# A hybrid decoder kernel: the attention norm's inverse square root is shared between GpSimd and VectorE, and the searches for the weight maxima are placed elsewhere

## The chip, the cores and the metric

The kernel runs on one core of a Trainium2 chip. The metric is the device time of one execution in microseconds (us); the median of several executions counts. The core has a matrix engine (TensorE, PE in the profile), VectorE (DVE), ScalarE (ACT), GpSimd (POOL), and SyncE (SP), which only issues transfers here. Every engine works through its own queue in order, and they wait for each other through semaphores.

## The reference, cut to what matters

Two layers, each with sliding-window attention (part A) and retention (part B) side by side, for 2048 prompt tokens and 8 x 4 sample tokens. What the change touches is the norm of the attention's queries and keys, and nothing else that is computed:

```
def rms_norm(x, g=None):
    y = xf * lax.rsqrt(jnp.mean(xf * xf, axis=-1, keepdims=True) + EPS)
...
    qa = rotary(rms_norm(qa.reshape(N, T, A_HEADS, A_HEAD_DIM), q_norm_g), pos, A_ROT_DIM, ROPE_THETA_A)
    ka = rotary(rms_norm(ka.reshape(N, T, A_KV_HEADS, A_HEAD_DIM), k_norm_g), pos, A_ROT_DIM, ROPE_THETA_A)
```

A token has 8 query heads and 2 key heads of 64 values, so ten means of squares per token: one number in each of ten columns, 128 tokens on 128 partitions. The weight maxima are not in the reference. The kernel splits each float32 matrix into two float16 parts (high and low) after scaling it by its largest absolute value, and needs that maximum before it can convert a block of weights.

## The kernel before, in words

A layer has four blocks of weights in this order: A (attention's projection), B0 and B1 (two retention heads each), and O (the output projection). Each block is one stage, and each stage runs over 17 steps: 16 tiles of 128 prompt tokens and one step of 32 sample tokens (step 0 in A, step 2 in the others). The order on every engine is written out by hand. Weights of the next block are searched for their maximum, scaled and converted on VectorE and ScalarE during the stage before, in eight rows of 128 x 1024 (1280 for A).

**An attention step on VectorE** is `a_step` (L1443). For tile s, with t = s - 1 and u = s - 2: the low halves of t's turned queries and keys (`a_lo`, L1022, the instruction at L1027 last), landing s's queries (`a_land_q`), low halves of u's probabilities (`a_plo`), masks and row maxima of t's scores (`a_softmax`, L1096), landing s's keys with the sums of squares (`a_land_k`, L972), and then s's norm, woven into the eight instructions that mix u's heads (`a_mix_head`, L1171). It ends with `a_rotate` (L1002: product with the norm at L1007, rotary to L1019), the gate (L1039), `a_plo` of t (L1053) and, from step 8 to 15, the low halves of one row of B0's weights (`w_low`, L924). TensorE needs L1027 for its scores (L640) and L1019 for its transposes (L604); SyncE turns the probabilities with a transposing DMA (`r<-r`, L2218) after `a_plo`.

**The norm's chain** has 12 links on VectorE, each waiting for the one before: mean plus epsilon (L994), then `rsqrt_link` (L877): an integer shift (L881, with x times -0.5 beside it, L882), the magic constant (L884), and three Newton rounds of three instructions (L886, L888, L890). In steps 0 to 2 the chain stands by itself (`a_norm`); from step 3 its links lie between the heads. `Chain` counts the links on a semaphore:

```
def __call__(self, ins):
    self.put(ins)
    self.wait()
```

**The weight maxima**: `w_absmax` (L901) reduces one row to a column (L907), `w_top` (L911) reduces the eight columns (L915, L918), GpSimd combines the partitions (`share_max`, L2109, the reduction at L2112), and `w_scale` (L927, from L931) makes the scales. In attention B0's rows are searched behind steps 4 (rows 0, 1), 5 (2 to 4) and 6 (5 to 7), with the top behind step 6 and the scales behind step 7. In retention the next block's rows are searched behind the gate of step 3 (rows 0 to 3), behind step 4 (4, 5) and behind step 5 (6, 7, and the top).

**A retention step on VectorE** is `b_step` (L1577): rotary (L1200 to L1211), decay of the scores (L1222), gate (L1039, which waits for ScalarE's tanh, L1831), state (L1264), norm and mix (L1274 to L1282). Around the sample step the order is written out (L1597 to L1610): rotary of the sample S, its gate, decay of T1, `b_vbd` (L1234), rotary of T2, state of T1, decay of S, mix of T1, gate of T2, four `w_absmax`, `b_sum` (L1241), state of S (L1254), mix of S. TensorE waits for L1254 before the scores of T2 (L704) and for L1222 before each output (L724).

**GpSimd's queue** holds the weight loads and the eight `share_max`. `attend` (L2120) issues B0's rows 0 to 3 at its c = 2 and rows 4 to 7 at c = 3, one straight after the other, as nothing stands between them; the c = 2 entry waits, in layer 0, for the eighth turned tile and, in both layers, for a piece count of VectorE that is reached by the end of the previous stage. `share_max` for B0 stands at c = 6.

Of the kernel before, what the change touches and what calls it, by code (L numbers as in the profile page):

```python
# [36 lines left out]
P = 128  # L37
# [25 lines left out]
RSQRT1_LINKS = 2 + 2 * NEWTON  # L63

# [133 lines left out]
def trunk(nc, x_prompt, x_sample, cache_k, cache_v, state_ret, w_in, w_out, norm_g, q_g, k_g, sinks,  # L198
          rope_ap, rope_as, rope_bp, rope_bs, mask_a, mask_s, decay, decay_s, cols, ident,
          y_p, y_s, nk_p, nv_p, nst_p, nk_s, nv_s, nst_s, mixed):  # L200
    with ExitStack() as ctx:
# [27 lines left out]
        ones = sb("ones", [P, KT])  # L229
        g_cur = sb("g_cur", [P, KT])  # L230
# [111 lines left out]

        ch_wm, ch_ws = sem("chain_w_max"), sem("chain_w_scale")
# [520 lines left out]
        def _(v):  # L864
# [12 lines left out]
            def rsqrt_link(ch, x, y, t, i):  # L877

                ch.wait()
                if i == 0:  # L880
                    ch.put(V.tensor_scalar(y.bitcast(I32), x.bitcast(I32), 1, None, ALU.logical_shift_right))  # L881
                    V.tensor_scalar(x, x, -0.5, None, ALU.mult)  # L882
                elif i == 1:
                    ch.put(V.tensor_scalar(y.bitcast(I32), y.bitcast(I32), -1.0, MAGIC, ALU.mult, ALU.add))  # L884
                elif i % 3 == 2:
                    ch.put(V.tensor_tensor(t, y, y, ALU.mult))  # L886
                elif i % 3 == 0:
                    ch.put(V.tensor_tensor(t, t, x, ALU.mult))  # L888
                else:
                    ch.put(V.scalar_tensor_tensor(out=y, in0=t, scalar=1.5, in1=y, op0=ALU.add, op1=ALU.mult))  # L890

# [80 lines left out]
            def a_land_k(L, s):  # L972

                r, b = s.rows, s.par
                ch = Chain(v, ch_an, 4 + RSQRT_LINKS, an(L, s))
# [13 lines left out]
            def a_norm_link(s, ch, i):  # L989

                r, b = s.rows, s.par
                if i == 0:
                    ch.wait()
                    ch.put(V.tensor_scalar(ss[0:r, :], ss[0:r, :], 1.0 / A_DIM, EPS, ALU.mult, ALU.add))  # L994
                else:
                    rsqrt_link(ch, ss[0:r, :], rs[0:r, b, :], rt[0:r, :], i - 1)

            def a_norm(s, ch):
                for i in range(RSQRT_LINKS + 1):
                    a_norm_link(s, ch, i)  # L1000
# [417 lines left out]
            def layer(L, last):  # L1418
# [4 lines left out]
                def a_first(s):  # L1423

                    if s.sample:
# [3 lines left out]
                        a_norm(s, ch)  # L1429
# [8 lines left out]
                    a_norm(s, ch)  # L1438
# [4 lines left out]
                def a_step(s, k=None):  # L1443
# [26 lines left out]
                    if not u.sample:  # L1470
                        a_mix_open(L, u, 0, m0)
                        a_mix_head(u, 0, 0)
# [48 lines left out]
                for c in range(CVA):  # L1521
# [954 lines left out]
```

## Time and profile before

| | before |
|---|---|
| three runs | 1908.94 us median (1907.4 to 1910.17) |
| the profiled execution | 1902.62 us, span of the core 1900.8 us |
| TensorE | 1750.4 us busy (92%) |
| VectorE | 1386.5 us busy (73%), 4768 instructions |
| ScalarE | 825.5 us busy (43%) |
| GpSimd | 68.5 us busy (4%) |
| TensorE's mean granted clock | 0.983 of full |

The profile is one execution; its rows are compared with its own time. A busy time says how long an engine had something running, a wait what it stood still for. In a timeline row the first number is the start, the second the time covered by the merged instructions (x4: four of them), and the brackets give the idle time before it and what ended it. `w_b`, `r`, `land`, `PA`, `TK` and the like are the program's buffers. A stage is found by its lines: attention runs to about 391 us and from 1008 to 1307 us; the four retention phases follow each of them.

### The profile page before, as it was taken

To read this page: it belongs to the slowest core of one execution; us is meant where nothing else is said; L and a number is where in the kernel's file an instruction comes from. 1 tells how busy PE (TensorE), PEld (TensorE's weight loads), DVE (VectorE), ACT (ScalarE), POOL (GpSimd) and SP (SyncE) were. 2 spreads that over 40 slices of the span, in tenths; PEclk is the share of its full clock that TensorE was granted. 3 is DMA by queue.
4 is the path that set the end of the run, shared out by engine and by line. 5 is a ranking of instruction groups with operands and counts; after the bars stand their busy time and mean duration, and the time that the engine had idled before them with its cause. 6 is when DMAs were issued, how large, how long until landed. Compare 5 with 4: busy or idle time off the path is not lost.

```text
span 1900.8 us, 35728 instructions
## 1 busy us (share of the span) xinstructions
PE 1750.4 (92%) x11512; PEld 947.5 (50%) x11512; DVE 1386.5 (73%) x4768; ACT 825.5 (43%) x1917; POOL 68.5 (4%) x108
## 2 busy tenths in 40 slices
PE   0778899999999999988998989999899999999999
PEld 0345555554555455543445555555455555555444
DVE  4768999987665766678875899998866676667442
ACT  2556566653443334332443556665344333442010
POOL 3010000000000000011001000000100000000000
PEclk9798999999999999999999999999999999999999
DMA  5874455466114211179893454554611143115774
GB/s 152 207 186 72 88 106 110 99 135 154 31 33 125 72 44 33 32 207 275 254 263 129 80 106 92 111 112 87 187 31 33 42 111 87 32 33 134 207 214 144
DMA packets 419520, 220.92 MB, mean 116 GB/s; under 512 B 360257, under 2 KB 391169, under 8 KB 419265
## 3 DMA queue, kind: packets, MB, share of 16 engines
q1 hardware_dynamic: 346336, 168.41, 36.7%
q0 software_dynamic: 9728, 35.66, 5.7%
q10 hardware_dynamic: 63360, 15.74, 5.0%
q8 instruction: 41, 0.67, 0.1%
q14 instruction: 55, 0.44, 0.1%
HBM read 88.75 MB, written 49.68 MB: 73 GB/s over the span
## 4 chain that ended last, share of the span: by engine, by line
PE 45%; DVE 31%; DMA 7%; ACT 6%; issue 5%; SPq 3%; ACTq 1%; DVEq 0%; POOL 0%
PE PB L550 19%; PE PA L550 19%; DMA r<-r 5%; DVE w_mx L907 3%; DVE r L1096 2%; DVE r L1053 2%; PE OB L724 1%; PE S L704 1%; DVE r L1200 1%; DVE mix L1171 1%; PE S L742 1%; PE OB L732 1%; DVE land L1039 1%; DVE r L1058 1%; DVE w_a L924 1%
## 5 line engine op out<-in xcount | busy, mean ns | idle before, releaser
L550 PE MATMUL PB<-w_a,hT 128*128 128x512 f16 (+1 forms) x1920 | 403.9, 363 | 0.0
L550 PE MATMUL PA<-w_a,hT 128*128 128x512 f16 (+1 forms) x1920 | 401.9, 360 | 0.0
L550 PEld LDWEIGHTS PB<-w_a,hT 128*128 (+1 forms) x1920 | 186.5, 99 | 182.4 <-issue 15.4
L550 PEld LDWEIGHTS PA<-w_a,hT 128*128 (+1 forms) x1920 | 185.9, 99 | 176.3 <-issue 5.4
L550 PE MATMUL PA<-w_b,r 128*128 128x512 f16 x768 | 172.7, 382 | 14.5 <-DMA r<-r 11.6
L1862 ACT ACTIVATE w_a<-land 128x1024 uint16<-128x1024 uint16 x60 | 63.4, 1057 | 279.4 <-DVE land L1211 267.8
L550 PE MATMUL PB<-w_b,hT 128*128 128x512 f16 x768 | 175.9, 379 | 0.3 <-DVE r L1200 0.3
L550 PE MATMUL PA<-w_b,hT 128*128 128x512 f16 x768 | 173.3, 381 | 0.0
L550 PE MATMUL PB<-w_b,r 128*128 128x512 f16 x768 | 171.3, 379 | 1.1 <-DVE r L1335 1.1
L1779 ACT ACTIVATE r<-r,nm,unqk 128x256 f32<-128x256 f32 x192 | 112.6, 588 | 45.5 <-DVE sd L1109 45.5
L550 PEld LDWEIGHTS PA<-w_b,r 128*128 128x128 f16 x768 | 74.5, 98 | 108.5 <-DMA r<-r 13.4
L550 PEld LDWEIGHTS PB<-w_b,r 128*128 128x128 f16 x768 | 74.8, 98 | 91.7 <-DVE r L1335 2.5
L550 PEld LDWEIGHTS PA<-w_b,hT 128*128 (+1 forms) x768 | 75.0, 99 | 85.5 <-issue 3.7
L550 PEld LDWEIGHTS PB<-w_b,hT 128*128 (+1 forms) x768 | 74.8, 98 | 83.5 <-DVE r L1200 0.4
L1039 DVE SCALAR_TENSOR_TENSOR land<-land,PB 128x256 f32<-128x256 f32 (+2 forms) x50 | 25.3, 505 | 106.3 <-ACT land L1831 101.2
L1888 ACT ACTIVATE r<-r,minv 128x1024 f16<-128x1024 f32 (+1 forms) x34 | 39.0, 1149 | 146.3 <-DVE minv L1296 138.3
L1851 ACT ACTIVATE r<-w_a 128x1024 uint16<-128x1024 uint16 x60 | 82.0, 1367 | 26.8 <-DMA w_a<-w_a 26.7
L1039 DVE SCALAR_TENSOR_TENSOR land<-land,PA 128x256 f32<-128x256 f32 (+3 forms) x52 | 26.6, 512 | 87.8 <-ACT land L1831 85.5
L576 PE MATMUL PA<-w_a,hT 128*32 128x256 f16 (+1 forms) x336 | 21.6, 339 | 55.0 <-DVE w_a L924 54.1
L1335 DVE SCALAR_TENSOR_TENSOR r<-PB,mdd,r 128x512 f32<-128x512 f32 x32 | 23.9, 748 | 62.2 <-PE PB L550 61.9
L724 PE MATMUL OB<-land,r 128*128 128x128 f32 x256 | 50.8, 283 | 13.7 <-DVE r L1222 13.5
L1709 ACT ACTIVATE w_b<-w_b,w_gs (+1 forms) x64 | 46.4, 725 | 23.0 <-DVE w_b L924 16.2
(268 smaller groups left out, 2858.0 us busy)
## 6 DMA issues: line engine op xcount, KB each, us to landing
out<-r SPq DMA_DIRECT2D x40, 512.0 KB, 4.7
r<-mixed SPq DMA_DIRECT2D x32, 512.0 KB, 4.2
w_b<-in_w_in POOLq DMA_DIRECT2D x16, 512.0 KB, 8.8
mixed<-mix SPq DMA_DIRECT2D x32, 256.0 KB, 2.0
mixed<-mix SPq DMA_DIRECT2D x64, 128.0 KB, 1.8
w_a<-in_w_in POOLq DMA_DIRECT2D x16, 512.0 KB, 7.8
w_b<-in_w_out POOLq DMA_DIRECT2D x16, 512.0 KB, 7.8
r<-in_x_prompt SPq DMA_DIRECT2D x16, 512.0 KB, 4.5
```

The source lines that it names most:

```text
L550: last = nc.tensor.matmul(out[0:s.rows, 0:n], lhs, w16(ph, k, p, wpart), start=(k == 0 and part == 0 and wpart == 0), stop=(k == KT - 1 an ...
L724: nc.tensor.matmul(ob[0:r, h * P:(h + 1) * P], stm[0:r, h * r:(h + 1) * r], v, start=True, stop=s.first)
L907: last = V.tensor_reduce(w_mx[:, k:k + 1], raw(L, kind, k), AX.X, ALU.max, apply_absolute_value=True)
L1039: V.scalar_tensor_tensor(out=th, in0=th, scalar=1.0, in1=src, op0=ALU.add, op1=ALU.mult).then_inc(dve_piece, 1)
L1053: V.scalar_tensor_tensor(out=ph16[0][:, 1, :], in0=r1[:, 1536:2560], scalar=P_TOP, in1=ph16[0][:, 0, :], op0=ALU.mult, op1=ALU.subtract).t ...
L1096: return V.tensor_tensor_reduce(out=prob_q[g][h // 2][:, h % 2 * 256:h % 2 * 256 + 256], in0=(SS, XX)[g][h // 2][:, (h % 2) * 256:(h % 2) ...
L1335: V.scalar_tensor_tensor(out=x, in0=bank("O", s, p)[0:r, :], scalar=mdd[0:r, b:b + 1], in1=x, op0=ALU.mult, op1=ALU.add).then_inc(dve_piec ...
L1709: A.activation(w16(kind, k, c, 0), raw(L, kind, k, c), ACT.Copy, scale=w_gs[:, run(k, 1)]).then_inc(w_hi, 1)
L1779: A.activation(x, x, ACT.Exp, scale=unqk[:, 0:1], bias=nm[:, g, h:h + 1], accum_out=rsum[:, g, h:h + 1])
L1851: last = A.activation(qkT.bitcast(U16).rearrange("p (n e) -> p e n", e=2), plT, ACT.Copy)
L1862: A.activation(pl, land[:, lpar(ph, s), 0:512].bitcast(U16).rearrange("p (n e) -> p e n", e=2), ACT.Copy).then_inc(b_pl, 1)
L1888: A.activation(mh_of(s)[0:r, 0, :], mxt[0:r, b, :], ACT.Copy, scale=minv[0:r, b:b + 1]).then_inc(o_hi, 1)
```

## The change

1. `rsqrt_link` goes. The norm's chain on VectorE has five links (`NORM_LINKS`): mean plus epsilon, x times -0.5, and one Newton round. The start value of that round is written by GpSimd: `root` waits for the first link, raises the ten means to the power -0.5 with a tensor_tensor against a column of -0.5, and VectorE's second link waits for it (`a_rt`).
2. In steps 3 to 16 the first link stands ahead of the four heads of group 0, the second behind them, the third behind `w_low`'s first half, and the last two between the heads of group 1.
3. `root` of step c is queued on GpSimd ahead of whatever `attend` has at c, for all 17 steps of both layers. So B0's loads of rows 0 to 3 stand behind the root of step 2, rows 4 to 7 behind the root of step 3.
4. B0's maxima: rows 0 to 3 behind step 4, 4 to 7 behind step 5, with the top there.
5. Retention: two rows behind step 3's gate, two between decay and gate of step 4 and one behind step 4, two between decay and gate of step 5 and one behind step 5. Beside the sample, T1's decay comes ahead of S's gate.

```
-                ch = Chain(v, ch_an, 4 + RSQRT_LINKS, an(L, s))
+                ch = Chain(v, ch_an, 3 + NORM_LINKS, an(L, s))
...
-            def a_norm_link(s, ch, i):
+            def a_norm_link(L, s, ch, i):
                 r, b = s.rows, s.par
+                x, y, t = ss[0:r, :], rs[0:r, b, :], rt[0:r, :]
+                ch.wait()
                 if i == 0:
-                    ch.wait()
-                    ch.put(V.tensor_scalar(ss[0:r, :], ss[0:r, :], 1.0 / A_DIM, EPS, ALU.mult, ALU.add))
-                else:
-                    rsqrt_link(ch, ss[0:r, :], rs[0:r, b, :], rt[0:r, :], i - 1)
+                    ch.put(V.tensor_scalar(x, x, 1.0 / A_DIM, EPS, ALU.mult, ALU.add))
+                elif i == 1:
+                    v.wait_ge(a_rt, an(L, s) + 1)
+                    ch.put(V.tensor_scalar(x, x, -0.5, None, ALU.mult))
+                elif i == 2:
+                    ch.put(V.tensor_tensor(t, y, y, ALU.mult))
+                elif i == 3:
+                    ch.put(V.tensor_tensor(t, t, x, ALU.mult))
+                else:
+                    ch.put(V.scalar_tensor_tensor(out=y, in0=t, scalar=1.5, in1=y, op0=ALU.add, op1=ALU.mult))
...
                     if not u.sample:
+                        a_norm_link(L, s, ch, 0)
                         a_mix_open(L, u, 0, m0)
-                        a_mix_head(u, 0, 0)
-                        a_norm_link(s, ch, 0)
-                        a_mix_head(u, 0, 1)
-                        a_norm_link(s, ch, 1)
-                        a_mix_head(u, 0, 2)
-                        a_norm_link(s, ch, 2)
+                        for h in range(3):
+                            a_mix_head(u, 0, h)
                         a_mix_head(u, 0, 3).then_inc(a_mx, 1)
-                        a_norm_link(s, ch, 3)
+                        a_norm_link(L, s, ch, 1)
                         if k is not None:
                             w_low(L, "B0", k, 0)
-                        a_norm_link(s, ch, 4)
-                        a_norm_link(s, ch, 5)
+                        a_norm_link(L, s, ch, 2)
                         a_mix_open(L, u, 1, m1)
                         a_mix_head(u, 1, 0)
-                        a_norm_link(s, ch, 6)
+                        a_norm_link(L, s, ch, 3)
                         a_mix_head(u, 1, 1)
-                        a_norm_link(s, ch, 7)
+                        a_norm_link(L, s, ch, 4)
                         a_mix_head(u, 1, 2)
-                        a_norm_link(s, ch, 8)
                         a_mix_head(u, 1, 3).then_inc(a_mx, 1)
-                        a_norm_link(s, ch, 9)
-                        a_norm_link(s, ch, 10)
-                        a_norm_link(s, ch, 11)
                         a_rotate(L, s, ch)
...
-                    if c in (4, 5, 6):
-                        for q in ((0, 1), (2, 3, 4), (5, 6, 7))[c - 4]:
+                    if c in (4, 5):
+                        for q in range(4 * c - 16, 4 * c - 12):
                             w_absmax(L, "B0", q)
-                    if c == 6:
+                    if c == 5:
                         w_top(L, "B0")
...
-                def b_step(ph, s, k=None):
+                def b_step(ph, s, k=None, rows=()):
...
                     b_decay(ph, L, s - 1)
+                    for q in rows:
+                        w_absmax(L, nxt, q)
                     gate(ph, L, s, 1, 256, 768)
...
                     b_rope(ph, L, S)
+                    b_decay(ph, L, T1)
                     gate(ph, L, S, 1, 256, 768)
-                    b_decay(ph, L, T1)
...
                     gate(ph, L, T2, 1, 256, 768)
-                    for q in range(4):
+                    for q in range(2):
                         w_absmax(L, nxt, q)
...
                     for c in range(4, CV0):
-                        b_step(ph, mid(c))
+                        b_step(ph, mid(c), rows=((2, 3), (5, 6))[c - 4] if c < 6 else ())
                         if c < 6:
-                            w_absmax(L, nxt, 2 * c - 4)
-                            w_absmax(L, nxt, 2 * c - 3)
+                            w_absmax(L, nxt, 3 * c - 8)
...
+            G.memset(half[:, :], -0.5).then_inc(a_hf, 1)
+            pool.wait_ge(a_hf, 1)
...
+            def root(L, s):
+                r = s.rows
+                alone(pool, ch_an, (3 + NORM_LINKS) * an(L, s) + 2)
+                G.tensor_tensor(rs[0:r, s.par, :], ss[0:r, :], half[0:r, :].broadcast_to([r, 10]), ALU.pow).then_inc(a_rt, 1)
...
                 for c in range(STEPS):
+                    root(L, Step(c))
```

## Rows read from the trace of the kernel before

**Rows 1.** The page, its fourth part: the chain that ended last, by engine.

```profile
PE 45%; DVE 31%; DMA 7%; ACT 6%; issue 5%; SPq 3%; ACTq 1%; DVEq 0%; POOL 0%
```

**Rows 2.** Windows, steady attention, layers 0 and 1: length, busy PE, PEld, DVE, ACT, POOL; clock.

```profile
249.70:320.82 71.12, 66.73 (x598) 39.73 (x597) 68.91 (x264) 50.24 (x126) 0.00 (x0) 1.00 0.51 104
...
1182.02:1286.98 104.96, 101.66 (x896) 58.92 (x895) 97.98 (x391) 69.13 (x182) 0.00 (x0) 1.00 0.50 105
```

**Rows 3.** Waits of TensorE, 165 to 391 us: total, times, longest.

```profile
PE S L640 <- DVE r L1027: 15.4, 9, 4.5
```

**Rows 4.** Waits of TensorE, 1164 to 1307 us.

```profile
PE OB L680 <- DMA r<-r: 3.3, 7, 1.1
```

**Rows 5.** Timeline of VectorE around the sample step of retention B0, layer 0.

```profile
436.85 4.59 DVE L907 TENSOR_REDUCE w_mx<-w_a 128x1 f32<-128x1024 f32 x4
...
451.07 0.42 DVE L1222 TENSOR_TENSOR r<-S,t_dec 128x256 f32<-128x256 f32 x1
455.04 0.42 DVE L1039 SCALAR_TENSOR_TENSOR land<-land,PB 128x256 f32<-128x256 f32 x1 [3.55 <-ACT land L1831]
```

**Rows 6.** Timeline of TensorE in the same stretch.

```profile
445.68 0.71 PE L704 MATMUL S<-r 128*128 128x128 f32 x4 [1.23 <-DVE r L1254]
...
451.55 0.49 PE L724 MATMUL OB<-land,r 128*128 128x128 f32 x2 [2.57 <-DVE r L1222]
```

**Rows 7.** Windows behind that stall, first and last of the four retention phases.

```profile
451.00:460.00 9.00, 8.45 (x37) 4.76 (x38) 4.93 (x24) 3.80 (x10) 0.00 (x0) 0.81 0.84 148
...
1574.00:1584.00 10.00, 9.58 (x42) 5.19 (x43) 5.85 (x25) 3.06 (x10) 0.00 (x0) 0.83 0.97 199
```

**Rows 8.** TensorE's wait in layer 1's attention, and the window around it.

```profile
1135.23 0.28 PE L640 MATMUL S<-kT_hi,r 64*128 64x256 f16 x2 [1.80 <-DVE r L1027]
...
1130.00:1145.00 15.00, 13.04 (x134) 8.28 (x133) 14.72 (x59) 8.41 (x23) 0.35 (x1) 1.00 0.54 105
```

**Rows 9.** Timeline of VectorE in attention step 9: the norm's links between the heads.

```profile
246.19 0.16 DVE L994 TENSOR_SCALAR ss<-ss 128x10 f32<-128x10 f32 x1
...
247.14 0.75 DVE L924 SCALAR_TENSOR_TENSOR w_b<-w_b,w_gs 128x512 f16<-128x512 f32 x1
...
247.80 0.16 DVE L888 TENSOR_TENSOR rt<-rt,ss 128x10 f32<-128x10 f32 x1
...
248.00 0.17 DVE L890 SCALAR_TENSOR_TENSOR rs<-rt,rs 128x10 f32<-128x10 f32 x1
248.09 0.28 DVE L1171 SCALAR_TENSOR_TENSOR mix<-TK,rr,land 128x64 f32<-128x64 f32 x1
...
248.28 0.16 DVE L886 TENSOR_TENSOR rt<-rs 128x10 f32<-128x10 f32 x1
...
249.70 0.83 DVE L1007 TENSOR_TENSOR land<-land,rs 128x640 f32<-128x640 f32 x1
```

**Rows 10.** Timeline of VectorE: four heads with nothing between them.

```profile
402.97 0.85 DVE L1171 SCALAR_TENSOR_TENSOR mix<-OB,rr,land 128x64 f32<-128x64 f32 x4
```

**Rows 11.** Timelines of GpSimd and VectorE: the partition maximum, first and third time.

```profile
41.70 1.04 POOL L2112 PARTITION_ALL_REDUCE w_am<-w_m  x1 [24.13 <-DVE w_m L918]
...
42.78 0.15 DVE L931 TENSOR_SCALAR w_q<-w_am 128x1 f32<-128x1 f32 x1 [0.26 <-POOL w_am L2112]
...
474.64 0.16 DVE L918 TENSOR_REDUCE w_m<-w_mx 128x1 f32<-128x8 f32 x1
...
475.01 0.35 POOL L2112 PARTITION_ALL_REDUCE w_am<-w_m  x1 [44.03 <-DVE w_m L918]
```

**Rows 12.** Chain of waits, transfers with start and length; the page's median to landing last.

```profile
110.84 5.00 DMA out<-land
...
1059.14 6.30 DMA r<-r
...
1221.11 4.63 DMA r<-r
...
mixed<-mix SPq DMA_DIRECT2D x64, 128.0 KB, 1.8
```

More of the change, by code:

```diff
@@ L63 @@
 RSQRT1_LINKS = 2 + 2 * NEWTON
+NORM_LINKS = 5
 CH_A = ((0, A_W), (A_W, 2 * KV_W), (A_W + 2 * KV_W, A_W))
@@ L229, in trunk @@
         ones = sb("ones", [P, KT])
+        half = sb("half", [P, 1])
         g_cur = sb("g_cur", [P, KT])
@@ L341, in trunk @@
         alone_count = sem("alone_count")
+        a_rt, a_hf = sem("a_roots"), sem("exponent")
         ch_wm, ch_ws = sem("chain_w_max"), sem("chain_w_scale")
@@ L875, in rsqrt @@
                     ch(V.scalar_tensor_tensor(out=y, in0=t, scalar=1.5, in1=y, op0=ALU.add, op1=ALU.mult))
-            def rsqrt_link(ch, x, y, t, i):
-                ch.wait()
[L880 to L888, printed above, removed]
-                else:
-                    ch.put(V.scalar_tensor_tensor(out=y, in0=t, scalar=1.5, in1=y, op0=ALU.add, op1=ALU.mult))
             def rsqrt1(ch, x, y, t):
@@ L987, in a_land_k, with a_norm @@
                 return ch
-            def a_norm_link(s, ch, i):
+            def a_norm_link(L, s, ch, i):
                 r, b = s.rows, s.par
+                x, y, t = ss[0:r, :], rs[0:r, b, :], rt[0:r, :]
+                ch.wait()
                 if i == 0:
-                    ch.wait()
-                    ch.put(V.tensor_scalar(ss[0:r, :], ss[0:r, :], 1.0 / A_DIM, EPS, ALU.mult, ALU.add))
-                else:
-                    rsqrt_link(ch, ss[0:r, :], rs[0:r, b, :], rt[0:r, :], i - 1)
-            def a_norm(s, ch):
-                for i in range(RSQRT_LINKS + 1):
-                    a_norm_link(s, ch, i)
+                    ch.put(V.tensor_scalar(x, x, 1.0 / A_DIM, EPS, ALU.mult, ALU.add))
[6 more added lines that the diff above has]
+                    ch.put(V.tensor_tensor(t, t, x, ALU.mult))
+                else:
+                    ch.put(V.scalar_tensor_tensor(out=y, in0=t, scalar=1.5, in1=y, op0=ALU.add, op1=ALU.mult))
+            def a_norm(L, s, ch):
+                for i in range(NORM_LINKS):
+                    a_norm_link(L, s, ch, i)
             def a_rotate(L, s, ch):
@@ L1428, in a_first @@
                         gate("A", L, s, 2, A_W, A_W + 2 * KV_W)
-                        a_norm(s, ch)
+                        a_norm(L, s, ch)
                         if L == 0:
@@ L1437, in a_first @@
                     ch = a_land_k(L, s)
-                    a_norm(s, ch)
+                    a_norm(L, s, ch)
                     a_rotate(L, s, ch)
@@ L1500, in a_step @@
                     else:
-                        a_norm(s, ch)
+                        a_norm(L, s, ch)
                         a_rotate(L, s, ch)
```

## The prediction

> **What bounds the kernel now.** I began with the chain that ended last: TensorE holds 45% of it and VectorE 31% [rows 1], so the bound changes by stage, and each part of the change has to be read in its own stage. The windows come next. In layer 0's steady attention VectorE is busy 68.91 of 71.12 us (four steps of 17.8 us) and TensorE 66.73: VectorE paces, with TensorE close behind, idle (71.12 - 66.73) / 4 = 1.1 us a step. In layer 1 TensorE idles (104.96 - 101.66) / 6 = 0.55 us a step and VectorE 1.2 [rows 2]. The waits name the partner: TensorE stood 15.4 us in nine steps before its scores for VectorE's L1027 [rows 3], and in layer 1 waits for turned probabilities [rows 4], whose transfer starts after VectorE's L1053, behind the norm. So time taken from the norm's chain reaches TensorE in both layers, at most by these idle times. Retention is TensorE's, except beside the sample step. There VectorE runs four row searches in a row [rows 5], and TensorE then stands 1.23 and 2.57 us for what comes behind them [rows 6]. Right after, TensorE's granted clock is 0.81 over 9 us and 0.83 over 10 us in the first and last of the four phases [rows 7]: part of the stretch went at 1.2 GHz in place of 2.4. Before it fell, the engine had stood 3.8 us in two waits. A wait of 1.80 us in attention left the clock at 1.00 [rows 8].
>
> **Retention, searches spread.** Four searches cover 4.59 us [rows 5], two half of it. Two fewer before `b_sum` bring everything behind them 2.3 us forward. TensorE's first wait (1.23) goes; it then reaches the second 1.23 earlier and is released 2.3 earlier, so it still stands 2.57 + 1.23 - 2.3 = 1.5 us [rows 6]. That is 2.3 us gained per phase, and TensorE has no other wait of weight in the next steps, so it keeps them: 4 x 2.3 = **9.2 us**. The two searches that move ahead of step 4's gate take 2.3 us, where VectorE stands 3.55 us for ScalarE [rows 5]: costed at nothing, that wait covers them; without it they would cost their 2.3. The one left behind each step replaces two. T1's decay ahead of S's gate shortens another short wait of TensorE, but VectorE's chain from there to the searches has the same instructions: nothing.
>
> **Retention, clock.** The longest wait is then 1.5 us, less than the 1.80 that left the clock alone [rows 6, 8]. The lost clock is 9 x 0.19 = 1.7 us in each phase (10 x 0.17 at the last) [rows 7]: 4 x 1.7 = **6.8 us**. Ends: nothing if it still falls, 6.8 if not; I take 6.8.
>
> **Attention, instructions.** From L994 to L1007 the step took 249.70 - 246.19 = 3.51 us [rows 9]. The new order over the same stretch, with no wait for GpSimd: link to head 0.09; four heads at (0.85 - 0.28) / 3 = 0.19 apart [rows 10], 0.77; link to `w_low` 0.08; `w_low` to link 247.80 - 247.14 = 0.66; then head 0.09, link 0.19, head 0.09, link 0.19, head 0.09, head 0.19, product 0.19 [rows 9]. The sum is 2.63, say 2.6: 0.9 us less. Eight small instructions leave, but those between heads cost little, since a head fills the time a link waits.
>
> **Attention, the new wait.** VectorE reaches link 1 at 0.86 us after link 0's start. GpSimd's answer comes after 475.01 - 474.64 = 0.37 us to be woken, the power itself, and 0.04 us back (42.78 - 41.70 - 1.04) [rows 11]. The trace has no power on GpSimd. The nearest rows are its reductions, 0.35 us usually and 1.04 the first time [rows 11], over one value per partition against ten here. I take the larger, since ten powers are more work than one maximum; ends 0.35 and, as nothing excludes it, twice 1.04 = 2.1. At 1.04 the answer is there at 1.45, a wait of 0.6 us; 0.3 us is left of each step's gain. Behind link 1 in VectorE's queue stand `w_low`, for which ScalarE's next conversion waits, and the heads of group 1; all come with the chain. The Trainium skill (GPSIMD Engine Reference, section 4.1, Engine selection) puts elementwise work on VectorE and has GpSimd about twice as slow for two inputs; an estimate by that page, from VectorE's 0.16 us, is 0.33 us and no wait, which is the first rival below and would bring the sum to its 32. The same page, section 2.1 (Instruction dispatch), has the first call of a freshly loaded kernel pay about 6 us; if that met the first power, it would cost some 5 us once, where the rows show 1.04 against 0.35, so 0.7 once.
>
> Layer 0: nine steps with TensorE waiting for L1027, 9 x 0.3, and the last ones in part: **3.5 us**. Layer 1: 13 steps x 0.3 = 3.9, under the 0.55 cap. With eight searches in two steps instead of three, the step without any is TensorE's and gives about 1 us of VectorE's time away: **3.0 us**. Layer 0 loses less, its searched steps being longer. Steps 0 to 2 have the chain bare: twelve links of 0.20 were 2.4, now 1.45 + 4 x 0.20 = 2.25; six steps, half on the path: **0.5 us**.
>
> **GpSimd's queue.** Seventeen powers a layer join the queue, 17 us and more apart, with nothing of weight behind them but the loads. The loads of rows 0 to 3 move behind step 2's root, rows 4 to 7 behind step 3's, and are searched one and two steps later, so both have over 17 us. Roots behind four load issues (3 us) come a step later and lose nothing. But the loads meet other transfers. In layer 0 the small stores (5.00 us, where small stores usually take 1.8) lose their company: up to 3.2 gained. The transposes of steps 2 and 3 gain company in both layers: 6.30 against 4.63 where disturbed, 1.7 each, up to 6.8 lost [rows 12]. Together I take **-1.5**, ends +3.2 and -6.8.
>
> **Sum**: 9.2 + 6.8 + 3.5 + 3.0 + 0.5 - 1.5 = 21.5 us. The profiled execution took 1902.6 us, under all three runs shown; 1902.6 - 21.5 = 1881.1 for it, and for the median 1908.9 - 21.5 = **1887.4 us**.
>
> **Rivals.**
> 1. *The power is short* (0.35 us or less): answer at 0.76, no wait. Layer 0 gives 9 x 0.9 + 1 = 9, layer 1 13 x 0.55 - 1 = 6, the bare chains 2.5; with retention and transfers 16.0 + 17.5 - 1.5 = 32.0: 1877. For it: the seven short reductions. Against: ten powers per partition. Chance 0.18.
> 2. *Only retention pays*, because the power takes about 1.4 us and eats the norm's gain (16.0 - 2.5 = 13.5: 1895), or the clock still falls after 1.5 us and the attention gain holds (14.7: 1894), or both (1902). Chance 0.24.
> 3. *GpSimd becomes the bound of attention*: every step waits for the power. Its place is link 1, its price (power + 0.41 - 0.86) - 0.9 in 28 steps; against 13 us from the rest it decides from 0.5 us a step, a power of 1.8 us. At 3 us it is 28 x 1.65 = 46 less 13: 1942, slower. For it: the trace shows no power, and VectorE has at most 1.2 us of idle a step to hide it. Against: nothing that GpSimd computes in the trace takes over 1.04. Chance 0.12.
> 4. *The edits cancel*, a power near 1.8 us: 1905 to 1912. Chance 0.05.
>
> **How the numbers follow.** The forecast (1883 to 1892) has 0.41. The range takes it, rival 1 and nearly all of rival 2: 1876 to 1901. A measurement of this kernel can tell about 0.2%, 3.8 us: faster 0.83, same 0.05, slower 0.12.
>
> **What would show it.** Right: in each retention phase TensorE's wait before L704 is gone, the one before L724 is near 1.5 us, and the clock in those windows is 1.00; the gate of step 4 waits about 1.3 us instead of 3.55. In attention the row of link 1 has under 0.7 us of idle with GpSimd as its end, L994 to L1007 takes about 3.2 us, and the waits for L1027 shrink by 0.3 a step. Wrong: a power over 1.5 us in GpSimd's rows and attention steps longer than 17.8; a clock below 1.00 behind the sample; transposes in steps 2 and 3 over 7 us with TensorE waiting for them.

## The result, and the profile after

The changed kernel took 1963.42 us (median of 4 runs, 1960.57 to 1966.04) against 1908.17 for the kernel before in the same series: a ratio of 1.0294, 95% interval 1.0277 to 1.0312. It is 55 us slower where 21.5 us were to be gained. The condition of the third rival, every attention step waiting for the power (chance 0.12), is the one that came about: link 1 waited in all 34 steps. Its price does not give 1963, though: costs that it did not have came on top. The profiled execution's span is 1958.8 us, its mean TensorE clock 0.974 (0.983 before).

The chain that ended last, by engine, from the page after: GpSimd held 0% of it [rows 1] and now holds 3%, by one line.

```profile
PE 47%; DVE 27%; DMA 8%; issue 6%; ACT 5%; POOL 3%; SPq 3%; DVEq 0%; ACTq 0%; POOLq 0%
```

Windows over the same steps as [rows 2], from product to product (length, busy PE, PEld, DVE, ACT, POOL, clock):

```profile
272.55:349.50 76.95, 68.89 (x591) 40.69 (x590) 65.84 (x233) 49.32 (x125) 7.80 (x4) 0.96 0.47 96
1237.95:1351.74 113.79, 102.17 (x898) 59.17 (x896) 93.40 (x343) 69.21 (x182) 11.71 (x6) 1.00 0.46 97
```

A step of layer 0 went from 17.78 to 76.95 / 4 = 19.24 us, one of layer 1 from 17.49 to 113.79 / 6 = 18.97. VectorE does less work than before (65.84 against 68.91) and idles 2.8 us a step. The timeline of VectorE over the norm's links, layer 0, with the new wait in brackets:

```profile
287.62 0.17 DVE L983 TENSOR_SCALAR ss<-ss 128x10 f32<-128x10 f32 x1
287.73 0.86 DVE L1167 SCALAR_TENSOR_TENSOR mix<-OB,rr,land 128x64 f32<-128x64 f32 x4
290.03 0.17 DVE L986 TENSOR_SCALAR ss<-ss 128x10 f32<-128x10 f32 x1 [1.44 <-POOL rs L2115]
290.12 0.74 DVE L912 SCALAR_TENSOR_TENSOR w_b<-w_b,w_gs 128x512 f16<-128x512 f32 x1
...
291.78 0.81 DVE L1003 TENSOR_TENSOR land<-land,rs 128x640 f32<-128x640 f32 x1
```

GpSimd's timeline in the same step:

```profile
287.97 1.95 POOL L2115 TENSOR_TENSOR rs<-ss,half 128x10 f32<-128x10 f32 x1 [17.29 <-DVE ss L983]
```

All 34 powers of the kernel, by line (durations minimum, median and maximum in ns, first and last start), the records of GpSimd's queue on that line and on the maximum's, and, last, on the maximum's in the kernel before:

```profile
L2115 POOL TENSOR_TENSOR rs<-ss,half x34: 1950/1952/2009, 75.6 to 1366.1; 128x10 f32<-128x10 f32 x32, 32x10 f32<-32x10 f32 x2
L2115 POOLq MODIFY_POOL_CONFIG  x8: 7/11/11, 68.4 to 1188.8; - x8
L2101 POOLq MODIFY_POOL_CONFIG  x10: 6/11/16, 41.5 to 1452.7; - x10
...
L2112 POOLq MODIFY_POOL_CONFIG  x2: 11/11/11, 41.6 to 41.6; - x2
```

GpSimd starts 0.35 us after link 0 (0.37 was taken), works 1.95 us, and link 1 starts 0.11 us later (0.04 was taken): 2.41 us in all. The sum had 1.45. From link 0 to the product it is 291.78 - 287.62 = 4.16 us, against 3.51 before and 3.2 forecast. That is 0.65 us of the 1.46 that a step got longer. The rest is a **second wait**, at the gate. Timelines of ScalarE and VectorE, one step earlier:

```profile
271.71 0.72 ACT L1698 ACTIVATE w_b<-w_b,w_gs 128x512 f16<-128x512 f32 x1 [2.20 <-DVE w_b L912]
...
274.77 0.67 ACT L1734 ACTIVATE land<-PA,cs_A 128x512 f32<-128x512 f32 x1
...
275.47 0.69 DVE L1035 SCALAR_TENSOR_TENSOR land<-land,PA 128x512 f32<-128x512 f32 x1 [1.09 <-ACT land L1734]
```

`w_low` stands behind link 1 in VectorE's queue. ScalarE waits for it before its next conversion (2.20 us; 0.72 in a step of before), with its exponentials and its tanh in line behind that, and VectorE then waits for the tanh. Over the kernel ScalarE stood 39.4 us for `w_low` (16.2 before).

**Four powers are late.** These are the first powers behind each partition maximum of A and B0. Timelines of GpSimd and VectorE around the first, of GpSimd before the second and of TensorE after it:

```profile
75.61 2.00 POOL L2115 TENSOR_TENSOR rs<-ss,half 32x10 f32<-32x10 f32 x1 [32.92 <-issue]
...
77.72 0.16 DVE L986 TENSOR_SCALAR ss<-ss 32x10 f32<-32x10 f32 x1 [9.49 <-POOL rs L2115]
...
233.24 0.96 POOL L2101 PARTITION_ALL_REDUCE w_am<-w_m  x1 [5.86 <-issue]
250.54 2.00 POOL L2115 TENSOR_TENSOR rs<-ss,half 128x10 f32<-128x10 f32 x1 [16.34 <-issue]
...
255.95 0.47 PE L607 MATMUL S<-eye,land 128*128 128x128 f32 x1 [6.17 <-DVE land L1015]
```

The windows around the second:

```profile
246.00:256.00 10.00, 3.83 (x19) 1.58 (x17) 3.24 (x14) 2.73 (x7) 2.00 (x1) 0.86 0.07 27
256.00:264.00 8.00, 8.00 (x60) 5.33 (x61) 7.75 (x23) 3.57 (x7) 0.00 (x0) 0.75 0.70 131
```

VectorE waited 9.49 us for a power of 2.00. The idle time before such a power is put down to "issue", not to VectorE: GpSimd was released and started only later. The records tell when. The first pair on L2115 stands at 68.4 us, 0.3 us behind the start of link 0, and the power starts 7.2 us after it. There is one pair before each of the four late powers and before five of the eight maxima (the first, and the first behind each run of powers). The kernel before had one pair only, at its first maximum, which started 0.1 us later. TensorE stood 6.17 us behind the second late power and went on at a clock of 0.75.

**One transpose is slow.** In layer 0's step 3, by the chain of waits:

```profile
144.91 14.30 DMA r<-r
```

The timelines of GpSimd and TensorE beside it:

```profile
145.85 3.03 POOL L524 DMA_DIRECT2D w_b<-in_w_in  x4
...
159.25 1.46 PE L683 MATMUL TK<-r 128*128 128x64 f16 x24 [15.34 <-DMA r<-r]
```

**Retention went nearly as forecast.** Timelines of VectorE and TensorE, with the waits behind the sample step in B0, then in B1 of layer 0, then in B1 of layer 1:

```profile
470.45 0.42 DVE L1035 SCALAR_TENSOR_TENSOR land<-land,PB 128x256 f32<-128x256 f32 x1 [1.42 <-ACT land L1820]
470.79 2.34 DVE L895 TENSOR_REDUCE w_mx<-w_a 128x1 f32<-128x1024 f32 x2
...
478.59 0.68 PE L707 MATMUL S<-r 128*128 128x128 f32 x4 [0.40 <-ACT r L1840]
483.24 0.49 PE L727 MATMUL OB<-land,r 128*128 128x128 f32 x2 [1.37 <-DVE r L1218]
...
685.92 0.49 PE L727 MATMUL OB<-land,r 128*128 128x128 f32 x2 [1.94 <-DVE r L1218]
...
1634.01 0.49 PE L727 MATMUL OB<-land,r 128*128 128x128 f32 x2 [1.95 <-DVE r L1218]
```

The windows behind these three waits:

```profile
484.00:494.00 10.00, 10.00 (x54) 5.14 (x53) 8.14 (x28) 3.23 (x9) 0.00 (x0) 1.00 0.57 144
684.00:694.00 10.00, 8.08 (x36) 4.52 (x37) 8.16 (x29) 2.93 (x9) 0.00 (x0) 0.83 0.75 196
1634.00:1644.00 10.00, 9.70 (x51) 5.19 (x51) 8.11 (x26) 3.93 (x10) 0.00 (x0) 1.00 0.73 198
```

The wait of 1.23 us for L1254 [rows 6] is gone; in its place TensorE stands 0.40 us for ScalarE in B0 (1.07 in layer 1) and not at all in B1. The second is 1.37 (2.57 before, 1.5 forecast), the gate of step 4 waits 1.42 (3.55 before [rows 5], 1.3 forecast). Behind 1.37 us the clock stayed at 1.00; behind 1.94 in B1 of layer 0 it fell to 0.83, behind 1.95 in B1 of layer 1 it did not. From a phase's first scores on TensorE to its last, the four phases are together 14.4 us shorter than before.

### The profile page after: what moved, and what is told of

Read it like the earlier page. It is cut to its first block, busy times and chain, and to the rows that moved or that the text cites. A ratio compares the mean times of both kernels' runs of the same rounds, so it can differ in the third digit from the quotient of the medians.

```text
span 1958.8 us, 35519 instructions
## 1 busy us (share of the span) xinstructions
PE 1758.4 (90%) x11512; PEld 951.1 (49%) x11512; DVE 1357.8 (69%) x4496; ACT 825.8 (42%) x1917; POOL 137.5 (7%) x143
## 4 chain that ended last, share of the span: by engine, by line
PE 47%; DVE 27%; DMA 8%; issue 6%; ACT 5%; POOL 3%; SPq 3%; DVEq 0%; ACTq 0%; POOLq 0%
PE PA L553 20%; PE PB L553 20%; DMA r<-r 4%; POOL rs L2115 3%; DVE r L1092 3%; DVE w_mx L895 2%; DVE r L1049 2%; PE S L707 1%; PE OB L727 1%; PE OB L735 1%; PE S L745 1%; DVE r L1054 1%; ACT w_a L1768 1%; SPq L2343 1%; DVE w_a L1092 1%
## 5 line engine op out<-in xcount | busy, mean ns | idle before, releaser
L553 PE MATMUL PA<-w_a,hT 128*128 128x512 f16 (+1 forms) x1920 | 406.6, 363 | 0.0
L553 PEld LDWEIGHTS PA<-w_b,r 128*128 128x128 f16 x768 | 75.4, 99 | 112.4 <-DMA r<-r 16.2
L2115 POOL TENSOR_TENSOR rs<-ss,half 128x10 f32<-128x10 f32 (+1 forms) x34 | 66.8, 1964 | 726.1 <-DVE ss L983 538.5
L1698 ACT ACTIVATE w_b<-w_b,w_gs (+1 forms) x64 | 46.4, 725 | 46.3 <-DVE w_b L912 39.4
```

Source lines behind the costliest of these rows:

```text
L553: last = nc.tensor.matmul(out[0:s.rows, 0:n], lhs, w16(ph, k, p, wpart), start=(k == 0 and part == 0 and wpart == 0), stop=(k == KT - 1 an ...
L1698: A.activation(w16(kind, k, c, 0), raw(L, kind, k, c), ACT.Copy, scale=w_gs[:, run(k, 1)]).then_inc(w_hi, 1)
L2115: G.tensor_tensor(rs[0:r, s.par, :], ss[0:r, :], half[0:r, :].broadcast_to([r, 10]), ALU.pow).then_inc(a_rt, 1)
```

## The experiments

Three costs had to be told apart (the power's duration, the four late starts, the slow transpose), and with them a fourth, the place of `w_low`. Each ratio is to the kernel before, run on the same chip beside it; the columns are edit, median, ratio and 95% interval.

| kernel | edit | us | ratio |
|---|---|---|---|
| changed kernel | | 1963.42 | 1.0294 (1.0277 to 1.0312) |
| loads_first | loads ahead of the powers | 1951.07 | 1.0233 (1.0210 to 1.0255) |
| after_late | `w_low` ahead of link 1 | 1944.15 | 1.0175 (1.0144 to 1.0206) |
| preload | idle power behind each maximum | 1936.45 | 1.0151 (1.0126 to 1.0175) |
| pre_loads | both repairs | 1925.72 | 1.0094 (1.0064 to 1.0123) |
| mult | multiply instead of power | 1917.42 | 1.0059 (1.0039 to 1.0079) |
| late_link | both repairs, `w_low` ahead of link 1 | 1894.96 | 0.9949 (0.9929 to 0.9970) |
| split | both repairs, power in two pieces | 1894.95 | 0.9928 (0.9898 to 0.9959) |
| split_late | split and late_link together | 1886.35 | 0.9901 (0.9866 to 0.9937) |
| ret_only | before, with the retention part | 1895.84 | 0.9950 (0.9929 to 0.9971) |
| ret_early | ret_only, `w_low` early | 1890.69 | 0.9912 (0.9889 to 0.9935) |
| newton2 | ret_only, two Newton rounds | 1879.30 | 0.9861 (0.9834 to 0.9887) |
| n2_early | newton2, `w_low` early | 1871.32 | 0.9799 (0.9775 to 0.9822) |

**ret_only**: the kernel before with the retention hunks of the change alone (four searches in a row become two; the others spread; decay of T1 ahead of the sample's gate).

```diff
-                    for q in range(4):
+                    for q in range(2):
                         w_absmax(L, nxt, q)
...
-                        b_step(ph, mid(c))
+                        b_step(ph, mid(c), rows=((2, 3), (5, 6))[c - 4] if c < 6 else ())
```

> The kernel before with the retention part of the change alone (searches spread, T1's decay first). Theory 1, that retention pays as its stage shows in the profile after (the four phases together 14.6 us shorter) and all of the loss is attention's: 1908.2 - 14.6 = 1893.6 us, with TensorE's granted clock 1.00 behind the sample step in at least three of the four phases. Rival, that the phases are shorter only because attention hands over later or in another order: within 4 us of 1908.

The ratio of 0.9950 is 9.5 us (5.5 to 13.5); 16.0 were forecast. TensorE's timeline, behind the sample step in B0 and B1 of layer 0:

```profile
448.65 0.49 PE L724 MATMUL OB<-land,r 128*128 128x128 f32 x2 [1.38 <-DVE r L1222]
...
651.44 0.49 PE L724 MATMUL OB<-land,r 128*128 128x128 f32 x2 [1.92 <-DVE r L1222]
```

The window behind the second:

```profile
652.00:662.00 10.00, 10.00 (x45) 5.24 (x44) 8.15 (x27) 3.36 (x10) 0.00 (x0) 0.83 0.76 197
```

From first to last scores on TensorE the four phases are 4.2, 2.9, 4.5 and 2.6 us shorter than before, 14.2 together. In this execution the clock recovered in both B0 phases and in neither B1: there the wait left over is 1.92, not 1.38, and 10 x 0.17 = 1.7 us stay lost. Without the clock's 3.4 us the searches gave 10.8, where 9.2 were forecast. The profiled execution was the fastest of the five, 1889.81 us, at a mean clock of 0.989 where the others had 0.983 to 0.986, so it may show more recovered phases than the median has. So the retention part is good, and all of the loss lies in attention.

**mult**: the changed kernel with a multiply of the same shape in the power's place. It leaves out the power, so the norm's factor is another number; all else stands.

```diff
-                G.tensor_tensor(rs[0:r, s.par, :], ss[0:r, :], half[0:r, :].broadcast_to([r, 10]), ALU.pow).then_inc(a_rt, 1)
+                G.tensor_tensor(rs[0:r, s.par, :], ss[0:r, :], half[0:r, :].broadcast_to([r, 10]), ALU.mult).then_inc(a_rt, 1)
```

> The changed kernel with GpSimd's power replaced by a product of the same shape and the same operands; the norm is then not the reference's inverse square root. Theory 1, the loss is the power's own 1.95 us and what it needs loaded on GpSimd: the instruction takes at most 0.5 us, VectorE's second link waits at most 0.1 us, the four waits of 8 to 9.5 us go, attention's steady steps are back under 17.8 us, and the whole is near 1908 - 14.6 - 10 = 1884 (1878 to 1896). Rival, the hand-over through GpSimd and its semaphores costs the time whatever it computes: waits of over 1 us stay and the time stays over 1940.

Timeline of VectorE in a steady step, GpSimd beside it, and link 1 of the first step:

```profile
277.72 0.17 DVE L983 TENSOR_SCALAR ss<-ss 128x10 f32<-128x10 f32 x1
...
278.61 0.16 DVE L986 TENSOR_SCALAR ss<-ss 128x10 f32<-128x10 f32 x1
...
280.36 0.81 DVE L1003 TENSOR_TENSOR land<-land,rs 128x640 f32<-128x640 f32 x1
...
278.08 0.20 POOL L2115 TENSOR_TENSOR rs<-ss,half 128x10 f32<-128x10 f32 x1 [17.50 <-DVE ss L983]
...
76.21 0.16 DVE L986 TENSOR_SCALAR ss<-ss 32x10 f32<-32x10 f32 x1 [7.71 <-POOL rs L2115]
```

Without a wait the stretch takes 280.36 - 277.72 = 2.64 us: the 2.63 of the forecast. So VectorE's instructions were counted right. The instruction took 0.20 us where the power takes 1.95, and yet the four first ones still cost VectorE 7.7, 6.6, 7.3 and 6.6 us. **What is late is not the power but any elementwise instruction of GpSimd behind a partition maximum.** At 1917 us it lies between the theory's 1884 and the rival's 1940. The kernel is 45 us faster than the changed one (0.0235 of 1907) and still slower than before, so the power's duration, with all that it brings about, is the largest cost but not the only one.

**preload**: one power on an idle column behind each maximum of A and B0, so that the late start falls where nobody waits.

```diff
+            def warm_up(j):
+                G.tensor_tensor(warm[:, j:j + 1], warm[:, 4:5], half[:, :], ALU.pow)
...
             share_max(0, "A")
+            warm_up(0)
...
                     if c == 6:
                         share_max(L, "B0")
+                        warm_up(2 * L + 1)
```

> The changed kernel with one idle power of a single column on GpSimd right behind the partition maxima of A and of B0 in each layer (four in all), so that what GpSimd loads for a power after a partition maximum is loaded while nobody waits. Theory 1, that the four first powers wait 6.7 to 7.6 us more than the others because something is loaded between the two kinds of instruction: the four waits fall from 8.3 to 9.5 us to 1.4 to 2.3 us, and the time falls by 20 to 28 us, to about 1939. Rival, that the first power of a stage is late for another reason (its queue, a transfer, the clock): waits and time stay as they are, 1963.

GpSimd's timeline behind the second maximum:

```profile
232.73 0.38 POOL L2102 PARTITION_ALL_REDUCE w_am<-w_m  x1 [6.08 <-issue]
239.89 0.59 POOL L2110 TENSOR_TENSOR warm<-warm,half 128x1 f32<-128x1 f32 x1 [6.79 <-issue]
242.34 1.97 POOL L2122 TENSOR_TENSOR rs<-ss,half 128x10 f32<-128x10 f32 x1 [1.86 <-DVE ss L984]
```

The idle power takes the 6.79 us on itself, and the one that counts starts at once. The maximum, too, starts 6.08 us late behind a power: GpSimd pays in both directions. The four waits fell from 8.3 to 9.5 us to 1.5 to 2.3, together 29 us, and the time fell by 1.0294 - 1.0151 = 0.0143 of 1907 us (about the median of before), 27 us: nearly all of the four waits was on the path.

**loads_first**: B0's eight rows loaded ahead of the powers, as in the kernel before.

```diff
-                    root(L, Step(c))
...
-                    if c == 2:
+                    if c == (2 if L == 0 else 0):
                         pool.wait_ge(dve_piece, L * PIECES + PIECE0["A"] + 1)
-                    if c in (2, 3):
-                        load_weights(G, "B0", L, range(4 * c - 8, 4 * c - 4))
+                        load_weights(G, "B0", L, range(8))
+                    root(L, Step(c))
```

> The changed kernel with B0's eight rows loaded ahead of the powers again, at their old times (layer 0: ahead of the power of step 2; layer 1: ahead of the power of step 0). Theory 1, that the transposing transfer of 14.3 us in layer 0's step 3 is slow because the rows 4 to 7 are loaded beside it: it falls to about 6, TensorE's wait of 15.3 us to about 7, and the time by 7 to 10 us, to about 1955. Rival, that it is the tile loads on the same queue and the later start alone: the transfer stays over 12 us and the time within 3 us of 1963.

Step 3's transpose in its chain of waits:

```profile
146.49 5.92 DMA r<-r
```

It takes 5.92 us instead of 14.30, and the time falls by 0.0061 of 1907, 12 us. The transfers had been forecast at 1.7 us for each disturbed transpose.

**pre_loads**: both repairs.

> The changed kernel with both repairs: one idle power behind each partition maximum (the four late powers start at once) and B0's eight rows loaded ahead of the powers (the slow transpose of step 3 goes). Theory (the two costs lie in different places and add): 1936.5 with the first alone, less the 12.4 that the second alone gave, 1924, a ratio near 1.010; what is left above the kernel with the retention part alone (1895.8) is 28 us, one us for each of 28 steps. Rival (the two share a stall in step 3, where the late power and the slow transpose met): nothing beyond the better one, 1935.

1.0094: the two add (0.0143 + 0.0061 = 0.0204, measured 0.0200). What is left is 0.0144 above ret_only.

**late_link**: as pre_loads, with one exchange in the queue of VectorE.

```diff
-                        a_norm_link(L, s, ch, 1)
                         if k is not None:
                             w_low(L, "B0", k, 0)
+                        a_norm_link(L, s, ch, 1)
                         a_norm_link(L, s, ch, 2)
```

> As pre_loads, with w_low's first half ahead of link 1 of the norm in VectorE's queue, in place of behind it. Theory of a second cost (w_low stands behind the wait for the power, so ScalarE's next conversion and then the gate come late, 1.1 us a step): in the 16 steps that have a w_low the gate's wait for ScalarE goes back to under 0.3 us and link 1's wait to 0.6 to 0.8, about 1.5 us a step less, 16 x 1.5 = 24: near 1900. Rival (the step is paced by the power alone; the order only moves the wait from one place to another): link 1's wait shrinks by w_low's 0.6 and the gate's stays, 16 x 0.6 = 10: 1914. If neither counts, 1924 as pre_loads.

0.9949: 0.0145 less, 28 us, which is more than either theory gave. VectorE's timeline in one step:

```profile
282.69 0.74 DVE L913 SCALAR_TENSOR_TENSOR w_b<-w_b,w_gs 128x512 f16<-128x512 f32 x1
284.22 0.17 DVE L987 TENSOR_SCALAR ss<-ss 128x10 f32<-128x10 f32 x1 [0.78 <-POOL rs L2122]
...
287.29 0.69 DVE L1036 SCALAR_TENSOR_TENSOR land<-land,PA 128x512 f32<-128x512 f32 x1
```

The window over four steps of layer 0:

```profile
250.19:320.69 70.50, 66.73 (x598) 39.78 (x596) 66.21 (x234) 50.25 (x125) 7.80 (x4) 1.00 0.52 104
```

The power takes its 1.95 us as before, but `w_low` now fills 0.66 us of it, ScalarE's tanh is on time, and the gate has no wait. A step is 70.50 / 4 = 17.62 us, against 17.78 in the kernel before. The exchange took 1.6 us off a step: 0.66 is the part of the power's wait that `w_low` fills, the rest the gate's wait. **With both repairs and this order, the power on GpSimd costs as much as it saves, within 0.003**: 0.9949 against 0.9950 for ret_only, which has no power at all. Even is the balance and not each step. By VectorE's products the steps from the first `w_low` on are 3.8 us shorter than in ret_only and those before 5.6 longer; in those the power's wait is uncovered, and B0's searches stand in two steps in place of three. No run separates these two.

**after_late**: the same exchange in the changed kernel, without the repairs.

> The changed kernel with one move only: w_low's first half ahead of link 1. Theory (the costs are separate: the order 31 us, the late first powers and the slow transpose the rest): 1963.4 - 31 = 1932, steady steps of 17.6 us in place of 19.2, the four late first powers (8 to 9.5 us) and step 3's slow transpose still there. Rival (the order only pays once the other two stalls are gone): over 1945.

0.0119 less, 23 us, with steady steps of 17.6. That is under the 28 us of the same move with the repairs, but within the intervals; at 1944 us it lies nearer the rival's number than the theory's. So that the costs simply add is not shown by this run. In its profile VectorE waited 24.7 us at step 3 for what the slow transpose held up, so that cost moves from run to run.

**split**: as pre_loads, with the power cut in two, the queries' eight columns raised as soon as their sums are there, the keys' two at the old place (VectorE's means are cut the same way).

```diff
+                alone(pool, ch_aq, 2 * an(L, s) + 2)
+                G.tensor_tensor(rs[0:r, s.par, 0:8], ss[0:r, 0:8], half[0:r, :].broadcast_to([r, 8]), ALU.pow).then_inc(a_rt, 1)
                 alone(pool, ch_an, (3 + NORM_LINKS) * an(L, s) + 2)
-                G.tensor_tensor(rs[0:r, s.par, :], ss[0:r, :], half[0:r, :].broadcast_to([r, 10]), ALU.pow).then_inc(a_rt, 1)
+                G.tensor_tensor(rs[0:r, s.par, 8:10], ss[0:r, 8:10], half[0:r, :].broadcast_to([r, 2]), ALU.pow).then_inc(a_rt, 1)
```

> As pre_loads, with the power cut in two: the eight columns of the queries are raised early, behind their sum and well ahead of the keys, and the two columns of the keys at the old place. Theory A (the power's time is work per column: 1.95 us for ten, so near 1.6 for eight and 0.4 for two): link 1's wait goes to 0 to 0.2 us in the steady steps, and the time comes to that of the kernel with the retention part alone or under it, 1885 to 1896. Theory B (the power's time is a cost per instruction, whatever the width): two columns take 1.9 us too, link 1 waits its 1.2 to 1.4 us as before, and VectorE has one more instruction a step: 1926 to 1930.

GpSimd's timeline of one step:

```profile
293.85 1.91 POOL L2132 TENSOR_TENSOR rs<-ss,half 128x8 f32<-128x8 f32 x1 [11.16 <-DVE ss L968]
300.04 0.70 POOL L2134 TENSOR_TENSOR rs<-ss,half 128x2 f32<-128x2 f32 x1 [4.28 <-DVE ss L993]
```

Theory B is out: two columns take 0.70 and not 1.9. Theory A holds for the ends: ten take 1.95, two 0.70, so (1.95 - 0.70) / 8 = 0.16 us a column and 0.4 fixed, and the one column of preload's idle power took 0.59 (4.08 the first time). By that eight should take 1.64. Eight of the 34 took 1.64 to 1.69, but the other 26 took 1.90 to 1.96, like ten; why is not shown. Link 1's waits summed to 10.9 us, and the kernel came to 0.9928. The gate still waited 1.1 us a step, as `w_low` stood behind link 1.

**split_late**: split with late_link's exchange.

> The two that came down to the kernel with the retention part together: the power cut in two (8 columns early, 2 late) and w_low's first half ahead of link 1, with both repairs. Theory (split alone still stood 1.1 us a step at the gate for ScalarE, late_link alone 0.5 to 0.8 at link 1; with both neither wait is left, and VectorE's chain is shorter than before by its eight instructions): steady steps of 17.2 in layer 0, 1880 to 1886. Rival (at 17.6 us TensorE or ScalarE is the bound, whichever wait of VectorE goes): 1890 to 1895, steps as in late_link.

VectorE's timeline at the gate of one step:

```profile
283.10 0.69 DVE L1045 SCALAR_TENSOR_TENSOR land<-land,PA 128x512 f32<-128x512 f32 x1 [0.88 <-ACT land L1745]
```

0.9901, the lowest with the power, with no wait left at link 1 in the steps that have a `w_low`. At 1886 us it is at the edge of the first theory, but not by its mechanism: the gate still waits 0.88 us (0.74 in layer 1), and the steady steps take 17.7 us, where 17.2 were expected and late_link has 17.6. Its interval overlaps split's, so a gain over split alone is not shown.

**newton2**: ret_only with two Newton rounds in the attention norm, which makes its factor less exact.

```diff
-                for i in range(RSQRT_LINKS + 1):
+                for i in range(RSQRT_LINKS - 2):
...
                         a_mix_head(u, 1, 3).then_inc(a_mx, 1)
-                        a_norm_link(s, ch, 9)
-                        a_norm_link(s, ch, 10)
-                        a_norm_link(s, ch, 11)
```

> The kernel before with the retention part, and two Newton rounds in the attention norm in place of three, all on VectorE: the last round of each is left out, GpSimd has no part. It measures what a shorter chain is worth when nothing new is waited for. The three links left out are the bare ones ahead of the product, 3 x 0.20 = 0.6 us a step. Theory (VectorE's chain paces the attention, up to TensorE's idle of 1.1 and 0.55 us a step): 0.5 us in each of 26 to 28 steps, 13 us: near 1883. Rival (TensorE takes the pace at once, since the chain is only now and then last): under 4 us, 1892 to 1896.

0.9861. VectorE's waits in layer 0, 245 to 325 us:

```profile
DVE land L1039 <- ACT land L1743: 4.0, 5, 0.8
```

The chain is 0.6 us shorter, and in these steps VectorE only comes 0.8 us too early to the gate. The gain of the medians (0.0089 of 1907, 17 us against ret_only) must come from other steps; the two profiled executions differ by 5.4 us only, so where it lies is not shown.

**n2_early**: newton2 with `w_low` ahead of the first group's heads.

```diff
+                        if k is not None:
+                            w_low(L, "B0", k, 0)
                         a_mix_open(L, u, 0, m0)
...
-                        if k is not None:
-                            w_low(L, "B0", k, 0)
                         a_norm_link(s, ch, 4)
```

> As newton2 (two rounds on VectorE), with w_low's first half ahead of the first group's heads, where it stood behind them. In newton2 VectorE stood 0.7 to 0.8 us a step at the gate for ScalarE's tanh, which it had not in the kernel with three rounds. Theory (that wait hangs on w_low's place, as in late_link): it goes, and the 16 steps with a w_low get up to 0.7 us shorter, of which TensorE's share lets half through: 1872 to 1876. Rival (w_low in front of the heads delays the outputs that they release by 0.66 us, so what the gate gains the heads lose): 1878 to 1882.

0.9799, the fastest of all, and ahead of both kernels. Windows over [rows 2]'s steps:

```profile
245.99:314.42 68.43, 66.73 (x598) 39.82 (x597) 66.99 (x253) 49.80 (x125) 0.00 (x0) 1.00 0.55 108
1182.02:1281.49 99.47, 98.31 (x890) 59.03 (x888) 93.99 (x372) 66.89 (x178) 0.00 (x0) 1.00 0.51 105
```

The gate's wait is gone, and TensorE idles 0.43 and 0.19 us a step. In layer 1 it is the bound; in layer 0 VectorE idles no more than it does, 0.36 us a step. So at most these 0.43 and 0.19 us a step are still to be had from VectorE.

**ret_early**: that move alone, with all three rounds kept.

> The kernel before with the retention part, all three Newton rounds kept, and w_low's first half ahead of the first group's heads. Theory (w_low's place only counts where VectorE stands at the gate for ScalarE; with three rounds it stands there 0.1 us a step): within 3 us of the kernel with the retention part alone, a ratio of 0.993 to 0.996. Rival (an earlier w_low helps ScalarE and through it the whole step, as two rounds with it gained 8 us over two rounds without): 6 to 8 us under it, a ratio of 0.990 to 0.992.

0.9912 (0.9889 to 0.9935) against 0.9950 (0.9929 to 0.9971) for ret_only. The point lies nearer the rival, but the intervals overlap: `w_low`'s place may be worth some microseconds even with three rounds, and this run does not settle it.

## Why the prediction was wrong, point by point

**Retention, searches (9.2 us)**: right in size, 10.8 in ret_only's profile. The wait behind the sample was forecast at 1.5 and came out at 1.38 in B0 and 1.92 in B1; the wait before the scores went, but in B0 one of 0.67 for ScalarE took its place. **Retention, clock (6.8)**: half right. I worked the wait out for one B0 phase and multiplied by four; B1's was left at 1.92, and the clock fell there in ret_only, twice. That takes 2 x 1.7 = 3.4 us off the 16.0 and leaves 12.6, inside ret_only's interval. In the profiles of all 13 kernels with the retention part, the clock stayed at 1.00 behind the sample in 25 of 26 B0 phases and in 13 of 26 B1 phases.

**Attention, instructions (0.9 us a step)**: right to 0.01 us, by mult.

**The power: the step that failed first.** I took 1.04 us from the first partition maximum, "since ten powers are more work than one maximum"; it took 1.95. The upper end of 2.1 held it, and rival 3 had its deciding point at 1.8. With 1.95 in the same formula a step loses 1.95 + 0.41 - 0.86 - 0.9 = 0.6 us, 28 x 0.6 = 17 us, less 13 from the rest: 1913, rival 4. So the mis-sized term explains a lost gain, and not 1963. The Trainium skill (GPSIMD Engine Reference, section 4.1, Engine selection) has GpSimd about twice as slow as VectorE for two inputs, by which the estimate was 0.33 us; mult's 0.20 us is under that, and the power is six times it. The Trainium skill's row there names add, multiply and maximum, and no power.

**What stood behind the wait: the second failed step.** I wrote that `w_low` and the heads "all come with the chain". They do, but `w_low` feeds ScalarE, and ScalarE's tanh feeds VectorE's own gate later in the same step. So one wait of VectorE made another one, and both were on the path: 0.0145 of 1907, 28 us, from pre_loads to late_link. The diff shows this placement in plain sight: `w_low` stood behind link 3 of a chain that had no wait, and stands behind link 1 of one that has.

**The late first powers: not priced.** I allowed 0.7 us, once. It came four times at 7 us more than the power itself, 27 us by preload. The Trainium skill (GPSIMD Engine Reference, section 2.1, Instruction dispatch) has the first call of a freshly loaded kernel pay about 6 us, and the trace agrees with the size: VectorE's four waits in mult are 6.6 to 7.7 us. I took "first" as once in a run. The rows show it each time that GpSimd goes from the partition maximum to an elementwise instruction (6.6 to 7.7 us from the record to the instruction, over all runs), and back (5.5 to 5.9). The trace of before could not show it, as GpSimd alternated there between the maximum and loads only.

**The transfers (-1.5, end -6.8)**: right in sign, too small. A transpose of step 3 took 14.3 us beside four loads of rows; 12 us by loads_first.

**The sum.** Above ret_only the changed kernel stands at 0.0344. Along one row of runs the late starts are worth 0.0143, the transpose 0.0057 (preload to pre_loads) and the placement of `w_low` 0.0145, each with an uncertainty of 0.003 to 0.004. That they come to 0.0345 says only that the row ends at late_link, and late_link measured the same as ret_only. The power's own 1.95 us, in a good place, costs as much as the eight instructions save. How much that is can be estimated from mult: 1.0059 less the late starts and the transpose, 0.0200, is 0.9859, which is 0.0091 or 17 us under ret_only, with an uncertainty of about 0.005. The first rival had 17.5 us for an attention without a wait.

## What to carry to other kernels

Before work is handed to another engine, price the very operation there, the trip (here 0.35 us to wake, 0.11 us back) and every change of kind in that engine's queue, and then follow what is queued behind the new wait until it comes back to the waiting engine. Work that another engine waits for should stand ahead of a new wait and not behind it: one exchanged line was worth 28 us here. And where a chain is too long, first ask whether a link can be dropped: one Newton round less on the same engine, with `w_low` early, beat every version that used a second engine, at the price of a less exact factor.

## What the runs showed of the hardware

- GpSimd's power over 128 partitions took 0.59 us for one column (about 4.1 the first time in a run), 0.70 for two, 1.64 to 1.69 or 1.90 to 1.96 for eight, and 1.95 for ten; a multiply over ten took 0.20.
- Between a partition maximum and an elementwise instruction 6.6 to 7.7 us passed from the MODIFY_POOL_CONFIG record to the instruction, and 5.5 to 5.9 us the other way, also where loads stood between the two; between a maximum and loads alone there was none.
- In the 13 profiles with the retention part, the waits of TensorE for the decay behind the sample were 1.92 to 1.95 us in B1, and the clock fell to 0.83 behind 13 of these 26. In B0 it stayed at 1.00 behind such waits of up to 1.75 us and fell behind the one of 1.86 (preload); behind one of 2.08 before the scores (n2_early) it stayed at 1.00. In attention it stayed at 1.00 behind 1.80 [rows 8]. So the length of the wait alone does not decide. Each of these clocks is that of the 10 us behind the wait, in one execution.
